# Attention of a streaming encoder layer: the values become the stationary operand, two heads in two column halves

## The reference

```
s = jnp.einsum('bnthd,bnmhd->bnhtm', q, kb).astype(jnp.float32) * (HEAD_DIM ** -0.5)
s = s + bias.astype(jnp.float32)[None, None]
s = jnp.where(key_valid[None, :, None, None, :], s, NEG_INF)
p = jax.nn.softmax(s, axis=-1).astype(vb.dtype)
return jnp.einsum('bnhtm,bnmhd->bnthd', p, vb)
```

## Time and profile before

| | |
|---|---|
| time, median of 3 runs | 2694.43 us (2690.66 to 2694.82) |
| span of the profiled execution | 2692.3 us |
| what the median has beyond that span | 2.1 us |
| PE busy | 2645.6 us, 98% of the span |
| DVE busy | 1750.8 us, 65% |
| ACT busy | 1362.9 us, 51% |
| attention stage | about 769 to 1074 us |
| in it: PE, DVE, ACT busy | 295.68, 188.75, 193.65 us of 305 |

### The profile page before, as it was taken

One profiled execution on the slowest core, in us unless ns is written; L12 is line 12 of the kernel. 1 busy time (PEld: TensorE's weight loads), 2 busy tenths in 40 slices (PEclk: granted clock), 3 DMA queues, 4 the chain that ended last, 5 costly groups with the idle time before them and its releaser, 6 DMA issues.

```text
span 2692.3 us, 50625 instructions
## 1 busy us (share of the span) xinstructions
PE 2645.6 (98%) x18664; PEld 1771.5 (66%) x18664; DVE 1750.8 (65%) x3367; ACT 1362.9 (51%) x2666; POOL 628.2 (23%) x698
## 2 busy tenths in 40 slices
PE   7999999999999999999999999999999999999998
PEld 2466666666668888557996666666666666666665
DVE  4966464655646666776778788888888875242433
ACT  4967474755656666113556555565555653121211
POOL 2600000000008889000000254433344311101000
PEclk9999999999999999999999999999999999999999
DMA  8621322031294442556552354445545438567572
GB/s 281 200 74 66 135 78 105 25 109 71 93 231 95 112 156 105 183 210 202 143 142 69 126 181 166 171 168 189 181 159 179 165 120 325 212 233 262 210 249 106
DMA packets 238419, 423.07 MB, mean 157 GB/s; under 512 B 57816, under 2 KB 162776, under 8 KB 230056
## 3 DMA queue, kind: packets, MB, share of 16 engines
q1 hardware_dynamic: 229400, 412.03, 46.1%
q10 hardware_dynamic: 8848, 8.74, 1.0%
HBM read 283.42 MB, written 139.92 MB: 157 GB/s over the span
## 4 chain that ended last, share of the span: by engine, by line
PE 84%; DVE 5%; ACT 4%; DMA 3%; issue 2%; POOL 1%; SPq 0%; DVEq 0%; ACTq 0%; POOLq 0%
PE ps L2988 57%; PE ps L3240 14%; PE ps L3080 4%; PE ps L3067 3%; PE ps L3056 2%; DMA arena<-in_w_mod_rest 2%; PE ps L2912 1%; ACT arena L1600 1%; PE ps L3094 1%; POOL arena L1140 1%; PE ps L3029 1%; DVE arena L2393 1%; DVE arena L2471 1%; ACT arena L1607 1%; DVE arena L2089 0%
## 5 line engine op out<-in xcount | busy, mean ns | idle before, releaser
L2988 PE MATMUL ps<-arena 128*128 128x352 f16 (+1 forms) x11880 | 1613.1, 297 | 5.1 <-ACT arena L1768 2.1
L2988 PEld LDWEIGHTS ps<-arena 128*128 128x128 f16 x11880 | 1100.6, 97 | 513.1 <-ACT arena L1768 2.5
L3240 PE MATMUL ps<-arena 128*128 128x352 f16 x2772 | 414.9, 310 | 0.5 <-DVE arena L2689 0.5
L3240 PEld LDWEIGHTS ps<-arena 128*128 128x128 f16 x2772 | 264.7, 96 | 150.8 <-issue 1.0
L1197 POOL TENSOR_TENSOR arena<-arena 128x128 f32<-128x128 f32 x44 | 30.6, 695 | 740.4 <-DMA arena<-in_w_down 740.1
L3094 PE MATMUL ps<-arena 128*128 128x424 f16 (+1 forms) x960 | 172.5, 341 | 2.1 <-DVE arena L2471 1.4
L1760 ACT ACTIVATE arena<-ps 128x352 f32<-128x352 f32 x264 | 116.3, 460 | 98.8 <-PE ps L2988 98.8
L1153 POOL CAST arena<-arena 64x512 f16<-64x512 f32 x8 | 4.9, 610 | 689.6 <-DMA arena<-in_cache_kT 689.3
L3080 PE MATMUL ps<-arena 128*128 128x64 f32 (+2 forms) x1200 | 151.0, 272 | 0.5 <-DVE arena L2435 0.5
L1207 POOL TENSOR_TENSOR arena<-arena 128x176 f32<-128x176 f32 (+1 forms) x57 | 56.2, 986 | 398.4 <-DMA arena<-ffn_hidden 398.4
L3080 PEld LDWEIGHTS ps<-arena 128*128 128x128 f32 (+2 forms) x1200 | 144.4, 193 | 3.4 <-issue 2.1
(11 more groups left out here) (239 smaller groups left out, 3587.1 us busy)
## 6 DMA issues: line engine op xcount, KB each, us to landing
hidden_combinations<-arena SPq DMA_DIRECT2D x48, 616.0 KB, 3.2
arena<-hidden_combinations SPq DMA_DIRECT2D x24, 1232.0 KB, 7.8
arena<-in_w_up SPq DMA_DIRECT2D x44, 512.0 KB, 4.9
down_combinations<-arena SPq DMA_DIRECT2D x44, 448.0 KB, 2.8
ffn_hidden<-arena SPq DMA_DIRECT2D x44, 440.0 KB, 3.1
arena<-down_combinations SPq DMA_DIRECT2D x10, 1792.0 KB, 7.8
arena<-down_combinations SPq DMA_DIRECT2D x20, 896.0 KB, 6.9
arena<-ffn_hidden SPq DMA_DIRECT2D x50, 352.0 KB, 3.9
```

Source lines behind the costliest of these rows:

```text
L2988: mm = pe.matmul(out, wt[:, k, wp, :], act_t[:, k, hp], start=(first and k == 0 and n == 0), stop=(last and k == K - 1 and n == 2), skip_g ...
L3240: mm = pe.matmul(ps[:, down_bank(n, k), 0:CF].rearrange("p (w t) -> p w t", w=2), dwt(i)[:, wi, wp, :], dact[i][:, :, bi, hp, :], start=(i ...
```

## The change

`outs` now keeps the values stationary (128 keys x 64 channels) and moves `pt` (128 query columns). The result comes out with channels on partitions, which is the layout that the merge wants: head 0 goes to partitions 0 to 63 and head 1 to 64 to 127 of one bank, and the matmuls of the two heads alternate. `outs` covers a tile (both heads) and is written in two parts, one for each step of `g`. `out_t` is gone. The row sums, which stood one to a partition, are needed along the columns now: the new `sums` multiplies the sums (stationary, spread over 64 columns) with the identity, into columns 128 to 255 of bank 1, and the new DVE step `inverse_sums` takes the reciprocal of the 128x128 result once for a tile. `out_n` is one 128x128 multiplication for a tile. `pt`, the sums and the bank of the result are doubled (by tile), and the stages behind `outs` come later by some steps of `g`.

The core of the diff:

```
-        pt = at_(46400, 2 * BAND).rearrange("p (h n) -> p h n", h=2)
-        osb = at_(47680, P)
+        pt = [at_(o, 2 * BAND).rearrange("p (h n) -> p h n", h=2) for o in (46400, 51776)]
+        osb, orec = at_(47680, P), [at_(o, P) for o in (53056, 53184)]
...
+        def out_cols(t):
+            return ps[:, 6 + t % 2, 0:P]
+
+        sum_cols = ps[:, 1, P:2 * P]
...
             def exps(x):
                 act.wait_ge(s_added, x.u + 1)
+                keep_above_zero(act, r_filled, x.tile - 1)
...
             def out_hi(x):
-                act.wait_ge(ot_filled, x.tile + 1)
-                act.activation(mixT[:, x.j, 0, x.q0:x.q0 + x.rows], ps[:, 7, 0:x.rows], ACT.Copy, scale=XS).then_inc(ot_hi, 1)
+                act.wait_ge(o_ready, x.tile + 1)
+                act.activation(mixT[:, x.j, 0, x.q0:x.q0 + x.rows], osb[:, 0:x.rows], ACT.Copy, scale=XS).then_inc(ot_hi, 1)
...
-            for g in range(NU + 3):
+            for g in range(NU + 6):
                 if 0 < g <= NU:
                     probs(Unit(g - 1))
                 if g < NU:
                     exps(Unit(g))
-                if g % 2 == 0 and g >= 4:
-                    out_hi(Unit(g - 4))
+                if g % 2 == 1 and g >= 7:
+                    out_hi(Unit(g - 7))
...
             def probs(x):
 
-                h = x.h
-                keep_above_zero(dve, o_ready, x.u - 1)
-                dve.wait_ge(p_ready, x.u + 1)
-                dve.reciprocal(rs[0:x.rows, h:h + 1], sm[0:x.rows, h:h + 1]).then_inc(r_ready, 1)
                 if x.w > 512:
                     k = min(P, x.w - 512)
                     dve.wait_ge(t_filled, x.u + 1)
-                    dve.tensor_copy(pt[0:k, h, 4 * P:5 * P], ps[0:k, 5, 0:P]).then_inc(t_dve, 1)
+                    keep_above_zero(dve, o_filled, x.tile - 1)
+                    dve.tensor_copy(pt[x.tile % 2][0:k, x.h, 4 * P:5 * P], ps[0:k, 5, 0:P]).then_inc(t_dve, 1)
+
+            def inverse_sums(x):
+                dve.wait_ge(r_filled, x.tile + 1)
+                keep_above_zero(dve, o_ready, x.tile - 1)
+                dve.reciprocal(orec[x.tile % 2][:, 0:x.rows], sum_cols[:, 0:x.rows]).then_inc(r_ready, 1)
 
             def out_n(x):
...
-                if h == 0:
-                    keep_above_zero(dve, ot_filled, x.tile)
-                dve.tensor_scalar(osb[0:rows, 64 * h:64 * h + 64], ps[0:rows, 6, 64 * h:64 * h + 64],
-                                  rs[0:rows, h:h + 1], None, ALU.mult).then_inc(o_ready, 1)
+                dve.wait_ge(o_filled, x.tile + 1)
+                dve.wait_ge(r_ready, x.tile + 1)
+                keep_above_zero(dve, ot_ready, x.tile)
+                dve.tensor_tensor(osb[:, 0:x.rows], out_cols(x.tile)[:, 0:x.rows], orec[x.tile % 2][:, 0:x.rows], ALU.mult)\
+                    .then_inc(o_ready, 1)
...
-            for g in range(NU + 3):
+            for g in range(NU + 7):
                 if g < NU:
                     scores(Unit(g))
                 if 0 < g <= NU:
                     probs(Unit(g - 1))
-                if 1 < g <= NU + 1:
-                    out_n(Unit(g - 2))
-                if g % 2 == 0 and g >= 4:
-                    out_lo(Unit(g - 4))
+                if g % 2 == 0 and g >= 8:
+                    out_lo(Unit(g - 8))
+                if g % 2 == 0 and 6 <= g < NU + 6:
+                    out_n(Unit(g - 6))
+                if g % 2 == 0 and 4 <= g < NU + 4:
+                    inverse_sums(Unit(g - 4))
...
+            def sums(x):
+
+                pe.wait_ge(p_ready, x.u + 2)
+                keep_above_zero(pe, s_added, min(x.u + 3, NU - 1))
+                keep_above_zero(pe, r_ready, x.tile)
+                for h in range(2):
+                    mm = pe.matmul(sum_cols[64 * h:64 * h + 64, 0:x.rows],
+                                   sm[0:x.rows, x.tile % 2, h:h + 1].to_broadcast([x.rows, 64]),
+                                   ident[0:x.rows, 0:x.rows], start=True, stop=True)
+                mm.then_inc(r_filled, 1)
+
+            def outs(x, part):
...
+                if part == 0:
+                    pe.wait_ge(t_act, x.u + 2)
+                    keep_above_zero(pe, t_dve, wide(x.u + 2))
+                    keep_above_zero(pe, o_ready, x.tile - 1)
                 nk = (x.w + P - 1) // P
-                for c in range(nk):
+                half = (nk + 1) // 2
+                for c in (range(half), range(half, nk))[part]:
                     k = min(P, x.w - c * P)
-                    mm = pe.matmul(ps[0:x.rows, 6, 64 * x.h:64 * x.h + 64], pt[0:k, x.h, c * P:c * P + x.rows],
-                                   vv[x.b][0:k, x.v0 + c, 64 * x.h:64 * x.h + 64],
-                                   start=(c == 0), stop=(c == nk - 1))
...
+                    for h in range(2):
+                        mm = pe.matmul(out_cols(x.tile)[64 * h:64 * h + 64, 0:x.rows],
+                                       vv[x.b][0:k, x.v0 + c, 64 * h:64 * h + 64],
+                                       pt[x.tile % 2][0:k, h, c * P:c * P + x.rows],
+                                       start=(c == 0), stop=(c == nk - 1), skip_group_check=True)
...
-            for g in range(-1, NU + 3):
+            for g in range(-1, NU + 4):
+                if g % 2 == 1 and 3 <= g < NU + 3:
+                    sums(Unit(g - 3))
                 if g + 1 < NU:
                     scores(Unit(g + 1))
...
+                if g >= 4:
+                    outs(Unit((g - 4) // 2 * 2), g % 2)
                 if 0 < g <= NU:
                     probs(Unit(g - 1))
-                if 1 < g <= NU + 1:
-                    outs(Unit(g - 2))
```

More of the change, by code:

```diff
@@ L164, in build @@
         pr = at_(45120, 2 * BAND).rearrange("p (h n) -> p h n", h=2)
-        pt = at_(46400, 2 * BAND).rearrange("p (h n) -> p h n", h=2)
-        osb = at_(47680, P)
-        mark, least, sm, rs = (at_(47808 + 2 * i, 2) for i in range(4))
+        pt = [at_(o, 2 * BAND).rearrange("p (h n) -> p h n", h=2) for o in (46400, 51776)]
+        osb, orec = at_(47680, P), [at_(o, P) for o in (53056, 53184)]
+        mark, least = (at_(47808 + 2 * i, 2) for i in range(2))
+        sm = at_(47812, 4).rearrange("p (b h) -> p b h", b=2)
         crow = at_(13056, 2 * D)
@@ L1599, in exps @@
                 act.wait_ge(s_added, x.u + 1)
+                keep_above_zero(act, r_filled, x.tile - 1)
                 act.activation(pr[0:x.rows, x.h, 0:x.w], pr[0:x.rows, x.h, 0:x.w], ACT.Exp, scale=-1.0,
-                               bias=least[0:x.rows, x.h:x.h + 1], accum_out=sm[0:x.rows, x.h:x.h + 1]).then_inc(p_ready, 1)
+                               bias=least[0:x.rows, x.h:x.h + 1],
+                               accum_out=sm[0:x.rows, x.tile % 2, x.h:x.h + 1]).then_inc(p_ready, 1)
             def probs(x):
                 act.wait_ge(t_filled, x.u + 1)
+                keep_above_zero(act, o_filled, x.tile - 1)
                 m = min(4, (x.w + P - 1) // P)
-                act.activation(pt[:, x.h, 0:m * P], ps[:, 4, 0:m * P], ACT.Copy).then_inc(t_act, 1)
+                act.activation(pt[x.tile % 2][:, x.h, 0:m * P], ps[:, 4, 0:m * P], ACT.Copy).then_inc(t_act, 1)
             def out_hi(x):
-                act.wait_ge(ot_filled, x.tile + 1)
-                act.activation(mixT[:, x.j, 0, x.q0:x.q0 + x.rows], ps[:, 7, 0:x.rows], ACT.Copy, scale=XS).then_inc(ot_hi, 1)
+                act.wait_ge(o_ready, x.tile + 1)
+                act.activation(mixT[:, x.j, 0, x.q0:x.q0 + x.rows], osb[:, 0:x.rows], ACT.Copy, scale=XS).then_inc(ot_hi, 1)
             def merge_hi(f):
@@ L3050, in scores @@
                 keep_above_zero(pe, s_added, x.u - 1)
+                if x.h == 0:
+                    keep_above_zero(pe, r_ready, x.tile - 2)
                 for bank, c in ((0, min(x.w, 512)), (1, x.w - 512)):
@@ L3069, in probs @@
                 mm.then_inc(t_filled, 1)
-            def outs(x):
-                if x.i == 0:
+            def sums(x):
[7 more added lines that the diff above has]
+                mm.then_inc(r_filled, 1)
@@ L3073, in outs @@
+            def outs(x, part):
+                if x.i == 0 and part == 0:
                     pe.wait_ge(values_loaded[x.b], x.b + 1 + 48 * (x.j // 2) + 48)
-                pe.wait_ge(t_act, x.u + 1)
-                keep_above_zero(pe, t_dve, wide(x.u + 1))
-                keep_above_zero(pe, o_ready, x.u)
+                if part == 0:
+                    pe.wait_ge(t_act, x.u + 2)
+                    keep_above_zero(pe, t_dve, wide(x.u + 2))
+                    keep_above_zero(pe, o_ready, x.tile - 1)
@@ L3085, in out_t @@
-            def out_t(x):
-                pe.wait_ge(o_ready, 2 * x.tile + 2)
-                keep_above_zero(pe, ot_ready, x.tile)
-                pe.transpose(ps[:, 7, 0:P], osb, ident).then_inc(ot_filled, 1)
+                    for h in range(2):
[3 more added lines that the diff above has]
```

(13 more changed lines are left out.)

20 lines of the change are left out of this document (5 added, 15 removed).

## The result

The changed kernel takes **2882.53 us** (median of 4 runs, 2878.17 to 2887.28) where the kernel before takes 2694.62 (4 runs, 2690.66 to 2697.49). The ratio is 1.0691, with a 95% interval of 1.0673 to 1.0709: 188 us slower. The profiled execution has a span of 2881.5 us, 189.2 above.

A forecast was written before the change was run, and what follows sets the result against it. PE's queue was taken to bound the attention stage, ACT close behind. Wait 94, narrow tiles 8, stage end 4 and clock 91 sum to 197 us on the 2692.3 span, with 2.1 for the median: 2890 us, range 2780 to 3000.

The forecast's parts named there:

- The wait: Ahead of `sums` on every wide tile, PE idles 1.9 us for the previous tile's reciprocal on DVE: 94 us.
- E: The point in PE's queue where PE is through with a step's transposes; the idle time was counted from it.
- PE's own work: PE's work for a wide tile: 4.4 us against 4.57 now, 0.1 to 0.2 us a tile won.
- The switches: Changes of weight width in PE's queue, into and out of `sums` and `outs` parts: six a tile, 0.12 us each.
- The overlap: In `outs`, the two heads' column halves run fully side by side: 1.2 us for 20 records.
- rival without overlap: In `outs`, halves don't overlap, about 1.0 us more a tile at full clock: 2940 to 2990; chance 0.15.
- Narrow tiles: The 16 narrow tiles get the reciprocal and the switches, 0.5 us each: 8 us.
- The clock: In the attention stage, PE's idle time lowers the granted clock for half of the wide tiles: 91 us.
- The end of the stage: Last reciprocal, `out_n`, `out_hi` and `out_lo` in a row, without the first merge product over them: 4 us.
- clock holds: In the attention stage, the wait is there but the clock stays at 1.00: 2800; chance 0.17.
- covered: Ahead of `sums`, DVE's reciprocal comes before PE asks, so the wait is mostly covered: 2720; chance 0.11.
- faster: Wait covered, switches cost 0.05, and PE's order runs free of ACT's and DVE's chains: 2676; chance 0.05.

The follow-up runs named there:

- e5: Changed kernel with `out_lo` moved behind the reciprocal on DVE, `osb` doubled, and `out_n` waiting for the `out_lo` of a tile earlier: 2792.11 us.
- e1: Changed kernel with the reciprocal (`inverse_sums`) moved on DVE to right behind the bias step, ahead of the copy of bank 5: 2705.22 us.
- e7: e1 with ACT's exponentials ahead of its copies of probabilities: 2697.83 us.
- e6: e1 with both heads' `outs` in the same 64 partitions, so one column half only (attention's result not computed): 2737.02 us.
- e3: Changed kernel with eleven unread matmuls of 384 columns ahead of each wide tile's `sums` (attention's result not fully computed): 2839.74 us.
- e10: Changed kernel with GpSimd's long modulation instructions cut to 8 columns (modulation's output left out): 2858.42 us.
- e8: Changed kernel rebuilt: sums in the result's bank, reciprocal and `out_n` ahead of the copy, `out_n` in place in PSUM, exponentials first on ACT: 2667.4 us.
- e12: e8 with `out_n` writing to two SBUF buffers in place of PSUM, which `out_hi` and `out_lo` read: 2681.34 us.
- e4: e1 with the `outs` loops exchanged, all chunks of head 0 and then all of head 1: 2721.32 us.

## Why the prediction was right

Predicted 2890 us, measured 2882.5; the direction, the mechanism and its place were right. That the two numbers lie within 8 us is luck: terms that were too small by some 40 us stood against one that was too large by as much and more.

- **The wait: right in place and count, near in length.** Predicted 1.9 us ahead of L3091, 52 times, until DVE's L2438: measured 1.96, 52 times. Two misses inside it cancel. The 0.20 from E to the copy was counted from the start of PE's next group, while PE's idle time begins with the end of the transposes, 0.02 us ahead of the copy. And copy, `out_lo` and `out_n` take 0.83 us and not 0.66, because `out_n` waits for the end of `out_lo`; e5 confirms that with a wait of 1.54. Odd step 4.2 predicted, 4.34 measured; even step 2.2 and 2.26; tile 6.4 and 6.60. e1 shows the cause: the reciprocal moved ahead of the copy, and 177 us are gone.
- **PE's own work: right in size, not in what it brings.** 4.4 us a tile predicted, 4.43 in e7. The switches were taken at 0.12; the differences of the chain are 0.11 (scores behind `sums`) and 0.15 (transposes behind `outs`). The 0.1 to 0.2 us a tile that PE would win never came out. It was reckoned against 4.57, which holds a wait of 0.1; the work itself was 4.47.
- **The overlap: right.** 1.2 us and a switch into each part for 20 records predicted, so 1.44; 0.59 + 0.81 = 1.40 in e7. e6 refutes the rival without overlap, with 2.47.
- **Narrow tiles: mis-sized a little.** 0.5 us each, 8 in all; their waits alone are 12.2.
- **The clock: the step that failed in size.** "I take half of them: 91 us", called a choice. e3 gives 43. The share of tiles was not too high, for 32 of 48 intervals are longer. The price was: 3.5 us stands for a whole tile at the lower level, and the clock is low in a part of it. In the tile from 797.30 the odd step costs 1.5 us more at 0.57, behind waits of 1.96 us, and the even step none, at 1.00. The mean of 0.81 lies just above the 0.65 to 0.8 given.
- **What is missing in the sum: `out_lo`.** It was counted at 0.22 us from the row of a kernel in which it read PSUM. The change gives it a second SBUF operand, and GpSimd works through most of the stage (236.54 of 305 us). e10 prices that at 24 us. The view of before showed the duration and could not show this dependence; the diff did, by `ps[:, 7, ...]` turning into `osb`.
- **The end of the stage: open.** No run prices its 4 us by itself.

Put together from measurements: 106 (52 tiles at 6.60 in place of 4.57) + 12 (waits of narrow tiles) + 21 (`out_lo` held up) + 43 (clock, e3) = 182, against 188. The 6 us left are not taken apart; the narrow tiles' own work, the end of the stage and a clock that e3 doesn't wholly restore are all in them. Beside the prediction's 94 + 8 + 4 + 91, the clock was 48 us too much, and the wide tiles lacked 12, the narrow ones 4 and `out_lo` all of its 21. The rival "clock holds", 2800, comes near what e3 shows: 2840, of which some 20 are the held `out_lo`. The rivals "covered" (2720) and "faster" (2676) come near e1, where `sums` finds its reciprocal done, and e8, where it waits for none and more was rebuilt than that.

## What to carry to other kernels

When a step is moved into another queue's order, write down what stands ahead of it there and which wait those have: here one reciprocal behind a copy that waits for PE's newest work cost 177 of 188 us, and the arithmetic that it belonged to was sound. Price an instruction anew when one of its operands moves between PSUM and SBUF, not only when its shape changes. And count a wait on TensorE at more than its length, with the clock as a term of its own, for the part of a tile in which it is low: shortening the waits by 53 us gave 90.

## What the runs showed of the hardware

- **A two-operand SBUF instruction of DVE waits for GpSimd.** 287 ns with one PSUM operand, 1039 with two in SBUF in the same program (e8, e12), 291 with two in SBUF when GpSimd's instructions are short (e10); up to 2.33 us in the changed kernel, until 0.14 us after the GpSimd instruction ended. SBUF — State Buffer in the Trainium skill, section "SBUF: two separate sides", says this: the shared port pair is an exclusive lock between a GpSimd operation and a DVE operation with two SBUF inputs. The runs agree, and the prediction had not applied it.
- **Column halves run side by side, somewhat out of turn.** Alternated, the records of the two heads start 6 to 8 ns apart at the upper clock (e1), and twelve of 128 f32 columns take 0.81 us, against 1.45 in one half (e6). Queued head after head, the second head's first record starts with three of the first head's still ahead of it, so eight records lose nothing and twelve lose 0.27 us (e4).
- **A switch of the weights' width** goes with 0.11 us more for the scores behind `sums` (64 columns) and 0.15 for the transposes behind `outs` (64) at the upper clock (e7). No run varies the width alone.
- **The clock with short gaps.** In a stage in which PE idles 2 us or more in every wide tile of 6.6 to 9 us the mean granted clock was 0.81, in turns at 1.2 and 2.4 GHz; with the gaps filled (e3), 0.96; with them shortened to 1.54 (e5), 0.90. 43 us of 188 were this.
